# Per-head norm factors spread over the partitions by one rounded product of a rounded part and a remainder

## What is computed

```python
def l2_normalize(x):
    return x * lax.rsqrt(jnp.sum(x * x, axis=-1, keepdims=True) + NORM_EPS)

def hybrid_mixer(h, norm_g, w_in, conv_w, ...):
    ...
    qkv = jax.nn.silu(depthwise_conv_centred(qkv, conv_w))
    q, k, v = jnp.split(qkv, [QK_WIDTH, 2 * QK_WIDTH], axis=-1)
    q = l2_normalize(q.reshape(bsz, seq_len, N_HEADS, HEAD_DK)) * (HEAD_DK ** -0.5)
    k = l2_normalize(k.reshape(bsz, seq_len, N_HEADS, HEAD_DK))
    ...
    o = jnp.moveaxis(o_fwd + o_bwd, 1, 2)[:, META_PAD:]
    o = rms_norm_2(o, out_norm_g) * jax.nn.silu(zf)
    y_d = o.reshape(bsz, seq_len, V_WIDTH) @ w_delta
```

## Time and profile before

| | |
|---|---|
| median of 3 runs | 1226.33 us |
| lowest and highest | 1221.73, 1238.04 us |
| profiled execution, its own time | 1235.44 us |
| its span | 1233.5 us |
| PE busy, matmul records | 1093.1 us (89%), 8281 |
| DVE busy, instructions | 490.2 us (40%), 957 |
| POOL busy, instructions | 383.4 us (31%), 175 |
| DMA in the last third | 425 to 429 GB/s |
| PE's granted clock, mean | 0.933 |

### The profile page before, as it was taken

The page is one execution under the profiler, slowest core; times in us unless marked ns, Lnnn a source line. Parts: engine busy times, 40 slices in busy tenths (PEclk is TensorE's granted clock), DMA queues, the critical chain, the costliest instruction groups (busy, mean ns, idle before and its releaser), DMA issues.

```text
span 1233.5 us, 20311 instructions
## 1 busy us (share of the span) xinstructions
PE 1093.1 (89%) x8281; PEld 871.4 (71%) x8281; DVE 490.2 (40%) x957; ACT 368.3 (30%) x552; POOL 383.4 (31%) x175
## 2 busy tenths in 40 slices
PE   9999999999999999999999999897666666777776
PEld 7999999999999868998789788554333333333333
DVE  4257835601146864548874421332211111111113
ACT  4554253443457642544333201200000000000001
POOL 4867577888876641641030000000000000000000
PEclk8999899999999988999999899998888888888898
DMA  6645355565555431423111384999999999999994
GB/s 225 204 127 157 117 156 170 174 187 185 180 165 193 148 111 35 129 78 137 69 71 69 147 364 174 381 425 429 426 429 428 427 428 428 427 429 427 427 412 173
DMA packets 41554, 304.37 MB, mean 247 GB/s; under 512 B 4869, under 2 KB 5253, under 8 KB 27786
## 3 DMA queue, kind: packets, MB, share of 16 engines
q1 hardware_dynamic: 41194, 302.82, 64.6%
q10 hardware_dynamic: 288, 0.52, 0.1%
HBM read 302.28 MB, written 1.05 MB: 246 GB/s over the span
## 4 chain that ended last, share of the span: by engine, by line
PE 60%; DMA 24%; DVE 12%; issue 2%; SPq 1%; ACT 1%; POOL 0%; DVEq 0%; ACTq 0%
DMA arena<-down 14%; PE bank L428 10%; PE bank L430 10%; PE bank L429 10%; DMA weights<-gate_up 7%; PE bank L794 6%; PE bank L1238 4%; PE bank L1255 4%; DMA arena<-gate_up 3%; DVE arena L2161 3%; PE bank L734 1%; PE bank L1209 1%; PE bank L1267 1%; DVE arena L2352 1%; DVE arena L2350 1%
## 5 line engine op out<-in xcount | busy, mean ns | idle before, releaser
L2717 POOL TENSOR_TENSOR rounded<-weights,rounded 128x1024 fp32r<-128x1024 f32 x152 | 368.9, 2455 | 194.3 <-ACT rounded L1332 182.2
L428 PE MATMUL bank<-rounded 128*128 128x256 f32 (+2 forms) x784 | 223.7, 285 | 0.7 <-POOL rounded L2717 0.7
L430 PE MATMUL bank<-rounded 128*128 128x256 f32 (+2 forms) x784 | 222.2, 283 | 0.0
L429 PE MATMUL bank<-rounded 128*128 128x256 f32 (+2 forms) x784 | 221.3, 282 | 0.0
L1332 ACT ACTIVATE rounded<-weights 128x1024 fp32r<-128x1024 f32 x146 | 147.1, 1052 | 112.2 <-PE bank L430 83.3
L428 PEld LDWEIGHTS bank<-rounded 128*128 128x128 f32 (+1 forms) x784 | 147.8, 188 | 2.9 <-POOL rounded L2717 1.2
L429 PEld LDWEIGHTS bank<-rounded 128*128 128x128 f32 (+1 forms) x784 | 148.3, 189 | 0.5 <-issue 0.2
L430 PEld LDWEIGHTS bank<-rounded 128*128 128x128 f32 (+1 forms) x784 | 147.1, 188 | 0.2
L428 PE MATMUL bank<-rounded,rounded 128*128 128x256 f32 (+2 forms) x456 | 133.0, 292 | 1.2 <-DVEq L2163 0.5
L430 PE MATMUL bank<-rounded,rounded 128*128 128x256 f32 (+2 forms) x456 | 130.4, 286 | 0.0
L429 PE MATMUL bank<-rounded,rounded 128*128 128x256 f32 (+2 forms) x456 | 130.0, 285 | 0.0
(11 more groups left out here) (439 smaller groups left out, 1399.0 us busy)
## 6 DMA issues: line engine op xcount, KB each, us to landing
weights<-front SPq DMA_DIRECT2D x152, 512.0 KB, 4.2
arena<-down SPq DMA_DIRECT2D x30, 2048.0 KB, 20.6
weights<-gate_up SPq DMA_DIRECT2D x28, 2048.0 KB, 33.4
arena<-gate_up SPq DMA_DIRECT2D x28, 2048.0 KB, 33.2
weights<-front SPq DMA_DIRECT2D x8, 2048.0 KB, 8.1
arena<-gate_up SPq DMA_DIRECT2D x4, 1536.0 KB, 32.9
weights<-gate_up SPq DMA_DIRECT2D x4, 1024.0 KB, 15.0
arena<-down SPq DMA_DIRECT2D x4, 1024.0 KB, 7.8
```

What stands on the lines that cost most here:

```text
L428: nc.tensor.matmul(out, a[0], b[1], start=start, stop=False)
L429: nc.tensor.matmul(out, a[0], b[0], start=False, stop=False)
L430: return nc.tensor.matmul(out, a[1], b[0], start=False, stop=stop)
L2717: nc.gpsimd.tensor_tensor(lo, raw[q % RAW], hi.bitcast(f32), ALU.subtract).then_inc(sem("w_lo"), 1)
```

## The change

The stationary operand of the spread becomes `two_rows_r`, rounded, with the 4 x 4 identity in rows 0 to 3 and again in rows 32 to 35 and zeros between; the moving operand, `rn2_r` or `o_rn_r`, has the rounded factors in rows 0 to 3 and the remainder in rows 32 to 35. One rounded product over 36 rows adds the two. For this VectorE gets, in each of the six rounds behind the reciprocal, a cast and a subtraction (`split_rows`), both linked; ahead of the first convolution two clears and two small casts; ahead of `out_factors(0)` two clears.

```diff
--- before.py
+++ after.py
@@ -15,6 +15,7 @@
 LEN = SEQ + META
 W1 = 512
 CW = W1 // P
+SPREAD = 36
 NH = 4
 TOPK = SEQ // 4
 IDX = 64
@@ -272,6 +273,9 @@
         fa0 = place(4 * 2 * P).rearrange("p (g c) -> p g c", g=4)
         yf_lo, yf_lo_r = chunked(both(4 * SEQ), 4)
         rn2 = place(LEN)
+        rn2_r = rounded(RING + top[0], LEN)
+        top[0] += LEN
+        assert top[0] <= ARENA
 
         top[0] = solve_at
         turned, pairs = lanes3(32), lanes3(32)
@@ -293,6 +297,10 @@
         o_sq = k_tok.rearrange("p t c -> p (t c)").rearrange("p (h t) -> p h t", h=HEADS)
         o_rn = [arena[:, zone + i * SEQ:zone + (i + 1) * SEQ] for i in range(2)]
         row_of = stat(7)
+        o_rn_r = [rounded(RING + zone + (2 + i) * SEQ, SEQ) for i in range(2)]
+        stat_at[0] += -(consts_at + 4 * P + stat_at[0]) % 8
+        two_rows_r = rounded(RING + consts_at + 4 * P + stat_at[0], 8)
+        stat(8)
         z_g, g_g = (ring[3][:, i * 2048:(i + 1) * 2048].rearrange("p (j k t) -> p j k t", j=4, k=2) for i in range(2))
         Z_AT = 1
         QUERIES_AT = 0
@@ -755,9 +763,9 @@
                     last = nc.tensor.matmul(f.bank[0:4, 0:n], row_of[:, 3 - h:7 - h], squares[:, h, 0:n], start=h == 0, stop=h == 3)
                 end(f, last)
 
-            def on_all(row4, h):
-
-                return ident[0:4, h:h + 1].to_broadcast([4, P]), row4
+            def on_all(rows_r, h):
+
+                return two_rows_r[0:SPREAD, h:h + 1].to_broadcast([SPREAD, P]), rows_r[0:SPREAD]
 
             def norms(kind, half, src_sem, n):
                 pe.wait_ge(sem("sqn"), src_sem)
@@ -768,7 +776,7 @@
                 pe.wait_ge(sem("ssn"), 2 * count)
                 for h in range(4):
                     f = begin(f"s{kind}{half}{h}")
-                    a, b = on_all(rn2[0:4, 0:n], h)
+                    a, b = on_all(rn2_r[:, 0:n], h)
                     end(f, nc.tensor.matmul(f.bank[:, 0:n], a, b, start=True, stop=True))
 
             def to_tokens(kind, half, src, ready, pools=(WK, WK, WK)):
@@ -1113,7 +1121,7 @@
                 for i in range(2):
                     f = begin(f"os{half}{i}")
                     for j in range(2):
-                        a, b = on_all(o_rn[half][0:4], 2 * i + j)
+                        a, b = on_all(o_rn_r[half], 2 * i + j)
                         last = nc.tensor.matmul(f.bank[:, j * SEQ:(j + 1) * SEQ], a, b, start=True, stop=True)
                     end(f, last)
 
@@ -2163,6 +2171,11 @@
                 dve.sem_inc(free[f.b], 1)
                 dve.sem_inc(sem(f"conv_{kind}"), 1)
 
+            def split_rows(x, rows_r):
+
+                link(nc.vector.tensor_copy(rows_r[0:4], x))
+                link(nc.vector.tensor_tensor(rows_r[32:36], x, rows_r[0:4].bitcast(f32), ALU.subtract))
+
             def factors(kind, half, n):
 
                 f = got(f"n{kind}{half}")
@@ -2173,6 +2186,7 @@
                 factors.count += 1
                 dve.wait_ge(sem("sdn"), factors.count)
                 link(nc.vector.reciprocal(rn, rn))
+                split_rows(rn, rn2_r[:, 0:n])
                 dve.sem_inc(sem("ssn"), 1)
             factors.count = 0
 
@@ -2184,7 +2198,11 @@
                 dve.sem_inc(sem(f"{kind}_done"), 1)
 
             link(nc.vector.memset(row_of, 0.0))
+            nc.vector.memset(rn2_r[0:SPREAD].bitcast(f32), 0.0)
             link(nc.vector.memset(row_of[:, 3:4], 1.0))
+            link(nc.vector.memset(two_rows_r[0:SPREAD].bitcast(f32), 0.0))
+            nc.vector.tensor_copy(two_rows_r[0:4, 0:4], ident[0:4, 0:4])
+            link(nc.vector.tensor_copy(two_rows_r[32:36, 0:4], ident[32:36, 32:36]))
             conv("k0", kT[:, 0, :], "k", 8, 0)
             f = got("abT")
             link(nc.vector.tensor_copy(ab_T[0:32, :], f.bank[0:32, 0:LEN]))
@@ -2492,6 +2510,7 @@
                 dve.sem_inc(sem("ss_o"), 1)
                 dve.wait_ge(sem("sd_o"), half + 1)
                 link(nc.vector.reciprocal(rn, rn))
+                split_rows(rn, o_rn_r[half])
                 dve.sem_inc(sem("ss_o"), 1)
 
             def out_gated(half):
@@ -2505,6 +2524,9 @@
                     link(nc.vector.tensor_tensor(o, o, z_g[:, j], ALU.mult))
                     dve.sem_inc(sem("y_delta"), 1)
 
+            for half in range(2):
+                last = nc.vector.memset(o_rn_r[half][0:SPREAD].bitcast(f32), 0.0)
+            link(last)
             out_factors(0)
             out_factors(1)
             out_gated(0)
```

## The result

The changed kernel takes 1238.35 us (median of 20 runs, 1235.26 to 1241.12), before 1226.28 us (20 runs, 1221.73 to 1238.06): ratio 1.0078, 95% interval 1.0055 to 1.0102. Forecast: 1233.7 us, 1223 to 1244, within 2%. All of this holds, but in part by luck: the sum behind it is too large, and the time that it was added to too small.

The account below looks back on a forecast made before the run. The prediction took the chain passing between PE and VectorE ahead of 769 us as the bound, with VectorE late around the spreads. Its terms summed to +7.4 us on the median 1226.33, giving 1233.7 us, range 1223 to 1244.

Parts of the forecast that it names:

- Setup: VectorE ahead of the first convolution: two clears, two small casts and a link add 3.2 us, ends 0.9 and 4.4.
- The one-column row: Profile row of a one-column VectorE operation amid a GpSimd stream, only 0.15 us; by it the setup costs 0.9 us.
- First key round: VectorE's first factor round of the keys: a linked cast and subtraction add 0.8 us in an unbroken run.
- The rival in which GpSimd holds it too: First key round: cast and subtraction wait 2 us each for GpSimd's stream; 1238 us, chance 0.1.
- Second key spread: Spread products of the keys' second half, where PE sets the pace: rounded products save 1.4 us.
- Queries: Two query factor rounds in VectorE's unbroken run add 1.6 us; PE's lower clock behind them adds 1.2, range 0 to 2.7.
- the clock term: PE's clock behind the query rounds, around 604 us: longer pauses lower it, adding 1.2 us, range 0 to 2.7.
- Output: Output's rounds and gated pairs: last pair 1.1 us later, PE's 3.6 us saving becomes waiting; +0.7 us, range -0.5 to +2.5.
- Fourier products: PE's wait ahead grows to 3.3 us, so the part still at high clock may slow: +1.3 us, range 0 to 2.6.
- that PE sets the pace after all: Whole kernel: all 9.2 us of PE's products come off, VectorE's additions are hidden; 1217 us, chance 0.12.
- The Fourier products keep the high clock: Fourier products take 12 to 13 us in place of 23, 10 us less; 1222 us, chance 0.08.
- The low clock that stays until 632 us: Pauses near 600 us tip PE to the low level until 632 us, doubling 26.5 us of work; 1257 us, chance 0.03.

Follow-up runs that it names:

- after_busy3: Changed kernel plus three plain products of 512 columns that nothing reads, in PE's wait ahead of the Fourier products; 1226.01 us, ratio to before 0.9963.
- before_busy1: Kernel before plus one plain 128x512 product that nothing reads, ahead of the Fourier products; 1222.53 us, ratio to before 0.9957.
- control_before: The kernel before, unchanged, run and profiled again; 1225.58 us, eight runs at 1222.6 to 1226.3 and four at 1233.0 to 1237.7.
- start_busy: after_busy3 with the clear and two small casts of two_rows_r moved to the start of the program; 1223.25 us, ratio to before 0.9957.
- after_busy_plain: Changed kernel with PE's spreads plain float32 again, VectorE's rounded parts made but unread, and two unread products ahead of the Fourier products; 1233.16 us.
- start_busy_no_output: start_busy with the output's factors spread by plain products as in the kernel before, without their cast and subtraction; 1221.57 us.
- after_early: Changed kernel with the clear and two small casts of two_rows_r moved ahead of the first layer's first residual sum; 1236.34 us.
- after_plain_pe: Changed kernel with PE's spreads plain float32 again, while VectorE still makes the rounded parts and remainders, which nothing reads; 1242.18 us.
- start_busy_key1_only: Changed kernel with rounded spread for the second key half only, setup at program start, two unread products ahead of the Fourier products; 1221.62 us, ratio 0.9951.

## Why the prediction was right, and where its steps failed

Between the two profiles the sum of the stretches rose by 366.75 - 363.96 = 2.8 us; I had 7.4. The medians tell the same when runs are compared whose Fourier products have the same level of the clock: after against the upper group of before 1238.35 - 1235.05 = 3.3 us, after_busy3 against before_busy1 3.5 us. For the profiled execution I had said 1242.8 us, and 1237.62 came. The forecast of 1233.7 is off by 4.7 us only because two errors stand against each other, a sum that is 4 to 5 us too large and a base, the median of before, that is 9 us below the level to which after belongs. That is luck, and so is the place inside the range: its lower end takes both spreads in full (-6 and -5), its upper end stops 8 us short of the +6 and +12 that it names.

- Setup: 3.2 taken, 4.06 measured (4.60 - 0.54). Both casts were held, the upper of my two ends. The one-column row misled me. The Trainium skill, "SBUF — State Buffer", section "Who interferes with whom", counts casts among the operations that can take the port pair that VectorE shares with GpSimd, and has the other engine blocked for the whole instruction. By that rule I had 4.4; the trace agrees with it here, 1.58, 2.34, 2.35, 2.34 and 2.32 us for 4 x 4 casts beside GpSimd. Why the one-column operation was not held, no run shows. The wait that grew was also another than I said, L714 in place of `gl`.
- First key round: 0.8 taken and measured. The rival in which GpSimd holds it too did not come (0.29 and 0.43 us), but only by its place: in after GpSimd's rows end at 437.16 us and begin again at 441.78, and the cast and the subtraction lie between, from 438.06 to 438.82. That its 1238 us came out is chance.
- Second key spread: -1.4 taken, -3.7 measured in the pair (94.23 to 90.51). Between runs that each had one low stretch in it (mean granted clock 0.98) the difference is 93.54 (before_busy1) - 91.75 (after_busy3) = 1.8, and 1.0 to 2.5 for the other such pairs; the rest is such low stretches, one in the profile of before and none in that of after (1.00), two in that of control_before (0.96) and in start_busy none (90.61). The stretch is PE's, and I priced the product alone.
- Queries: 1.6 for the rounds and 1.2 for the clock taken, 2.15 measured, and 2.13 to 2.19 in every profile with this part (after_busy_plain aside, where PE is late), whatever the clock did there. It is two rounds of some 0.76 us and 0.63 us by which one cast was held, as the timeline of after shows (L2176 and GpSimd's clear beside it); the cast of the first query round took 0.28 us. The clock fell as I had said (the first product of `query_unit` took 2.08 us in place of 1.16), but it cost nothing: the clock term was 0, and the hold was missing from my sum.

```profile
597.27 0.91 DVE L2176 CAST rounded<-arena 4x256 fp32r<-4x256 f32 x1
```

```profile
597.09 0.95 POOL L2757 MEMSET arena<- 128x1024 f32 x1 [19.29 <-ACTq L1668]
```

- Output: +0.7 taken, -0.4 measured (+1.06 to the last gated pair, as said, then -1.5 behind it). The pair mixes clocks: up to the last gated pair the mean granted clock was 0.78 before and 0.87 after. At nearly the same clock, start_busy less start_busy_no_output, it is 71.62 - 70.85 = +0.8, and leaving the output out won 1.7 us of the median: the 0.7 was about right, and the -0.4 is the clock's. That "the 3.6 us that PE saves turn into waiting" is borne out by the waits of 1.53, 1.10 and 0.60 us.
- Fourier products: 1.3 taken, range 0 to 2.6; 0.03 in the pair and some 9 of the 12.1 us in the median. **This is the step that failed.** I read the low clock of the profiled execution as the state of the kernel before, and added the sum to a median that is mostly of runs at the high level. The range of the runs, 1221.73 to 1238.04, had the two groups in it. What the longer wait did (1.02 to 3.17 us) was not to lengthen the low stretch but to make it certain: none of the 44 runs of after, after_early and after_plain_pe lies under 1234.1 us, none of the 96 of the eight kernels with fill products (after_busy_plain with its slower PE aside) above 1229.8.

The rivals: that PE sets the pace after all was wrong for the change as made, yet its products are worth 7.1 us where VectorE carries the rounds; what decides is that both work on one chain, alternating. "The Fourier products keep the high clock" was given 0.08 as an event of the changed kernel; it describes the kernel before in over half of its runs. The low clock that stays until 632 us did not come.

So where do the medians' 12.1 us come from? About 3 are instructions (3.3 and 3.5 us, above), and the other 9 are that before is in the lower group in over half of its runs and after never. Taken one at a time, the fill takes off 12.3 us, the setup at its right place 2.8, the rounds of queries and output 1.4 and 1.7. These do not simply add: together they would leave 1220.2 us, and start_busy_key1_only, which has the fill, the setup at its right place and no round of the queries, the output or the first key half, is at 1221.62. The best version, start_busy_no_output at 1221.57 us, is 1.7 us below the lower group of before beside it (20 runs, median 1223.26; resampling gives 0.1 to 3.5): what it gains on the median of before comes mostly from the clock.

## What to carry to other kernels

Look at all times before a profile is trusted as "before": where the runs fall in two groups, find out which one the profile is of and what the other does, and price a change for each. A wait of 1 us ahead of a run of plain float32 products on TensorE went with a loss of some 10 us in 57 of 125 runs, a wait of 1.8 or 3.2 us in all 44, and a few products that nothing reads, placed in the wait, took that back. A small operation is not cheap if it stands in VectorE's unbroken run beside a stream of GpSimd that holds it, and moving it into idle time helps only if the idle time is as long as the hold.

## What the runs showed of the hardware that I had not expected

- TensorE's clock can fall or stay on the same rows: after the same thin products and the same wait of 1.0 us the Fourier products ran at 0.50 for 23.4 us in one profile and at 1.00 for 13.5 us in another, and over the 125 runs of before beside these experiments 57 are of the upper group. The Trainium skill, "TensorE: Matmul & The Clock Gate", section "Part 1: The HAM clock gate (the "warmup" mystery)", says that a busy engine comes back to the full clock; in the low stretch the records give PE as busy for 23.00 of 23.00 us, and it did not come back before the Fourier products had ended (471.5 us in before; the granted clock is 1.00 again from 474.2). What these products (plain float32, pairs of them over 16 rows) lack for it no run here tells apart.
- A cast of 4 x 4 numbers took up to 2.35 us beside GpSimd, and a clear of 36 x 8 numbers at the same place 0.07 us.
- Rounded products over 36 rows with a broadcast operand follow each other like those over 128 rows, 0.12 us apart: four take 0.76 us. The work that is added for it on VectorE, 0.29 + 0.43 us a round, is more than half of what PE saves, 1.3 us.
